# A transformer layer with 32 experts on one core: the test for further rounds turned round, and the second expert pair's work in another order

## What is computed

```python
def moe(h, w_router, b_router, w_up, b_up, w_down, b_down):
    ...
    top_vals, top_idx = lax.top_k(logits, TOP_K)          # 4 of 32 for each of 256 tokens
    wts = jax.nn.softmax(top_vals, axis=-1)
    ...
    def expert(acc, xs):
        wu, bu, wd, bd, g = xs
        gu = x @ wu + bu                                   # 1024 -> 2 x 1024
        gate, up = gu[:, :D_FF], gu[:, D_FF:]
        gate = jnp.minimum(gate, SWIGLU_LIMIT)
        up = jnp.clip(up, -SWIGLU_LIMIT, SWIGLU_LIMIT)
        glu = gate * jax.nn.sigmoid(SWIGLU_ALPHA * gate)
        y = ((up + 1.0) * glu) @ wd + bd                   # 1024 -> 1024
        return acc + g[:, None] * y, None
```

## Time and profile before

| | |
|---|---|
| runs | 1178.0, 1182.4, 1183.23 us; median 1182.4 us |
| profiled execution | 1181.97 us |
| its span, first to last instruction | 1180.2 us |
| TensorE busy | 1072.3 us (91%) |
| mean DMA rate over the span | 389 GB/s, 459.64 MB |
| mean granted TensorE clock | 0.979 of full |

### The profile page before, as it was taken

How to read it: one execution, slowest core, us unless ns; L and a number is a source line. 1 busy time by engine, 2 the same in 40 slices (tenths; PEclk the granted TensorE clock), 3 DMA queues, 4 the chain that set the end, 5 groups by cost and what they waited for, 6 DMA issues and landing times.

```text
span 1180.2 us, 13193 instructions
## 1 busy us (share of the span) xinstructions
PE 1072.3 (91%) x5399; PEld 505.3 (43%) x5399; DVE 304.6 (26%) x585; ACT 141.4 (12%) x275; POOL 43.2 (4%) x79
## 2 busy tenths in 40 slices
PE   7989999999999989898989898989898989898985
PEld 5755798554343333333333334333333343434321
DVE  3043867632212111111121211111212111212124
ACT  2013333111011010101010101010101010101011
POOL 2005000000000000000000000000000000000000
PEclk8999999999999999999999999999999999999998
DMA  9988564899999999999999999999999999999993
GB/s 331 407 304 274 192 257 138 345 422 385 429 427 430 428 427 429 429 429 428 427 428 429 429 428 428 429 428 429 429 428 429 429 429 428 428 429 422 420 421 123
DMA packets 51248, 459.64 MB, mean 389 GB/s; under 512 B 4444, under 2 KB 4504, under 8 KB 20648
## 3 DMA queue, kind: packets, MB, share of 16 engines
q1 hardware_dynamic: 49960, 455.12, 92.7%
q0 software_dynamic: 1024, 3.29, 1.0%
q10 hardware_dynamic: 224, 0.69, 0.2%
HBM read 457.51 MB, written 1.57 MB: 389 GB/s over the span
## 4 chain that ended last, share of the span: by engine, by line
PE 63%; DMA 32%; DVE 2%; issue 1%; SPq 1%; ACT 1%; POOL 0%; DVEq 0%; POOLq 0%; ACTq 0%
DMA ring<-in_w_down_dram 30%; PE ps L1605 17%; PE ps L1620 10%; PE ps L1555 6%; PE ps L1508 5%; PE ps L1519 5%; PE ps L1261 4%; PE ps L1475 2%; PE ps L1640 2%; PE ps L1548 1%; PE ps L1277 1%; PE ps L1535 1%; PE ps L1292 1%; PE ps L1294 1%; PE ps L1293 1%
## 5 line engine op out<-in xcount | busy, mean ns | idle before, releaser
L1605 PE MATMUL ps<-ring,arena 128*64 128x512 f32 x1664 | 364.8, 593 | 18.6 <-DMA ring<-in_w_up_dram 18.6
L1620 PE MATMUL ps<-ring,arena 128*64 128x512 f32 x896 | 212.8, 631 | 51.6 <-DMA ring<-in_w_down_dram 51.6
L1605 PEld LDWEIGHTS ps<-ring,arena 128*64 128x64 f32 x1664 | 121.3, 137 | 245.5 <-issue 243.2
L1620 PEld LDWEIGHTS ps<-ring,arena 128*64 128x64 f32 x896 | 73.5, 145 | 190.5 <-issue 169.6
L1115 DVE TENSOR_TENSOR arena<-ps,arena 128x512 f32<-128x512 f32 x64 | 44.0, 692 | 281.4 <-PE ps L1519 281.4
L1096 DVE TENSOR_SCALAR arena<-ps 128x512 f32<-128x512 f32 x32 | 20.6, 687 | 278.2 <-PE ps L1605 221.6
L1555 PE MATMUL ps<-ring,arena 128*64 128x512 f32 x368 | 80.8, 594 | 0.3 <-DMA ring<-in_w_up_dram 0.3
L1508 PE MATMUL ps<-arena 128*128 128x128 f32 x512 | 63.3, 282 | 0.0
L1508 PEld LDWEIGHTS ps<-arena 128*128 128x128 f32 x512 | 61.6, 196 | 1.8 <-issue 1.6
L1519 PE MATMUL ps<-arena 128*128 128x512 f32 x128 | 57.8, 594 | 1.2 <-ACT arena L716 1.2
L703 ACT ACTIVATE arena<-arena 128x512 f32<-128x512 f32 x32 | 19.6, 629 | 296.2 <-DVE arena L1096 296.2
(11 more groups left out here) (235 smaller groups left out, 801.7 us busy)
## 6 DMA issues: line engine op xcount, KB each, us to landing
ring<-in_w_up_dram SPq DMA_DIRECT2D x127, 2048.0 KB, 26.9
ring<-in_w_down_dram SPq DMA_DIRECT2D x63, 2048.0 KB, 23.1
ring<-in_w_in_dram SPq DMA_DIRECT2D x16, 1024.0 KB, 9.9
ring<-in_w_ada_dram SPq DMA_DIRECT2D x16, 1024.0 KB, 10.3
ring<-in_w_ada_dram SPq DMA_DIRECT2D x16, 512.0 KB, 11.8
ring<-in_w_out_dram SPq DMA_DIRECT2D x4, 1024.0 KB, 10.4
ring<-in_w_pa_dram SPq DMA_DIRECT2D x2, 1024.0 KB, 10.5
ring<-in_w_pb_dram SPq DMA_DIRECT2D x2, 1024.0 KB, 6.1
```

What stands on the lines that cost most here:

```text
L1605: ins = mm(ps[CAP * a:CAP * a + CAP, n, :], xgT[:, h, kk, CAP * a:CAP * a + CAP], w[a][:, n * HALF:(n + 1) * HALF], start=False, stop=(kk ...
L1620: ins = mm(ps[CAP * a:CAP * a + CAP, YB + n, :], hT[:, f, CAP * a:CAP * a + CAP], w[a][:, n * HALF:(n + 1) * HALF], start=(f == 0), stop=( ...
```

## The change

Two things are changed.

1. **The test for further rounds, on TensorE alone.** `further_rounds(pe, ...)`, four last products after it, becomes `finish(r)`: `If(flag < 1)` the last products (`last_scatter`), `Else` another round and `finish(r + 1)`. The other four engines keep their tests as they were.
2. **The first two pairs' order.** The second pair's `gather` leaves `up_first`. Its first half stands between the pairs, its second half before k-block 2 of the second pair. That pair's k-blocks 0 and 1 come before its bias: block 0 starts the banks (`start=first`), and the bias adds to them. `turn_hidden` moves from ahead of k-block 2 to ahead of k-block 3, `scatter(R)` from ahead of the bias to ahead of k-block 5, `turn_weights` from ahead of k-block 3 to ahead of k-block 7. On ScalarE the copy of the gather's second half moves behind the first pair's sigmoids.

```diff
-                for b in range(2):
-                    xg_out(R + 1, b, 1, SECOND[b])
+                xg_out(R + 1, 0, 1, SECOND[0])
                 sigmoids(R)
+                xg_out(R + 1, 1, 1, SECOND[1])
...
-                    if kk == 5:
-                        for b in range(2):
-                            gather(R + 1, b, SECOND[b])
...
+            def up_second(Q, chunk):
+
+                pe.wait_ge(u_read, Q + 1)
+                for kk in range(KB):
+                    if kk % 4 == 0:
+                        pe.wait_ge(xg_ready, Q * 2 + (kk // 4 + 1))
+                    if kk == 2:
+                        gather(Q, 1, SECOND[1])
+                        up_bias(Q, False)
+                    if kk == 3:
+                        pe.wait_ge(xg_ready, Q * 2 + 2)
+                        turn_hidden(Q - 1, FIRST_HB)
+                    if kk == 5:
+                        pe.wait_ge(hTe_ready, Q * 2)
+                        scatter(Q - 1)
+                    if kk == 7:
+                        turn_weights(Q - 1)
+                    up_block(1, kk, both_experts(chunk(kk), 2 * FF), kk == 0).then_inc(moe_free, 1)
...
-                pe.wait_ge(xg_ready, R * 2 + 4)
-                scatter(R)
-                up_by_block(R + 1, at(N + FIRST_UP), True)
+                gather(R + 1, 0, SECOND[0])
+                up_second(R + 1, at(N + FIRST_UP))
...
-                pe.wait_ge(woT_ready, 1 + (r + 1) * PAIRS)
-            further_rounds(pe, more, run)
-            pe.wait_ge(woT_ready, 1 + PAIRS)
-            for n in range(4):
-                t, c = n // 2, slice((n % 2) * HALF, (n % 2 + 1) * HALF)
-                pe.wait_ge(yg_ready, n + 1)
-                mm(ps[:, SB + n, :], woT[:, t, :], yg[:, t, c], start=True, stop=True).then_inc(last_scat, 1)
+
+            def last_scatter(r):
+                pe.wait_ge(woT_ready, 1 + r * PAIRS)
+                for n in range(4):
+                    t, c = n // 2, slice((n % 2) * HALF, (n % 2 + 1) * HALF)
+                    pe.wait_ge(yg_ready, n + 1)
+                    mm(ps[:, SB + n, :], woT[:, t, :], yg[:, t, c], start=True, stop=True).then_inc(last_scat, 1)
+
+            def finish(r):
+                if r == ROUNDS:
+                    last_scatter(r)
+                else:
+                    with pe.If(more[r - 1] < 1):
+                        last_scatter(r)
+                    with pe.Else():
+                        run(r)
+                        finish(r + 1)
+
+            finish(1)
```

More of the change, by code:

```diff
@@ L1540, in both_experts, with up_bias @@
                 return [v[:, a * 2 * FF:a * 2 * FF + n] for a in range(2)]
-            def up_bias(Q):
+            def up_bias(Q, first=True):
                 pe.wait_ge(u_read, Q + 1)
@@ L1548, in up_bias, with up_block @@
                         mm(ps[CAP * a:CAP * a + CAP, n, :], selbuf[:, a, :], bparts[:, n * HALF:(n + 1) * HALF],
-                           start=True, stop=False)
-            def up_block(h, kk, w):
+                           start=first, stop=False)
+            def up_block(h, kk, w, first=False):
                 for n in range(4):
@@ L1555, in up_block @@
                         ins = mm(ps[CAP * a:CAP * a + CAP, n, :], xgT[:, h, kk, CAP * a:CAP * a + CAP],
-                                 w[a][:, n * HALF:(n + 1) * HALF], start=False, stop=(kk == KB - 1))
+                                 w[a][:, n * HALF:(n + 1) * HALF], start=first, stop=(kk == KB - 1))
                 return ins
@@ L1574, in up_first, with up_last @@
                         up_block(0, kk, [spare[:, a, :] for a in range(2)]).then_inc(first_used, 1)
-            def up_by_block(Q, chunk, first):
+            def up_second(Q, chunk):
[15 more added lines that the diff above has]
+                    up_block(1, kk, both_experts(chunk(kk), 2 * FF), kk == 0).then_inc(moe_free, 1)
+            def up_last(Q, chunk):
                 pe.wait_ge(xg_ready, Q * 2 + 2)
-                if not first:
-                    pe.wait_ge(hTe_ready, Q * 2)
+                pe.wait_ge(hTe_ready, Q * 2)
                 up_bias(Q)
                 for kk in range(KB):
-                    if first and kk == 2:
-                        pe.wait_ge(acc_done, (Q - 1) * 4 + 2)
-                        turn_hidden(Q - 1, FIRST_HB)
                     if kk == 3:
-                        if first:
-                            pe.wait_ge(hTe_ready, Q * 2)
                         turn_weights(Q - 1)
@@ L1687, in experts @@
                 Q, n0 = R + PAIRS - 1, n0 + PC
-                up_by_block(Q, at(n0), False)
+                up_last(Q, at(n0))
                 pe.wait_ge(acc_done, Q * 4)
```

## The result

The changed kernel takes 1173.06 us (median of 6 runs, 1172.27 to 1174.36), the kernel before 1181.54 us (median of 6, 1178.0 to 1183.78). The ratio is 0.9926, 95% interval 0.9911 to 0.994: 0.74% faster, 8.7 us by the ratio and 8.5 by the medians. The profiled execution takes 1174.36 us against 1181.97, 7.6 us less.

A forecast was written before the change was run, and what follows sets the result against it. From about 300 us the stream of weights was taken to set the time. 1181.97 less 5.3 (branch) and 2.3 (order) gave 1174.4 us for the profiled execution; median forecast 1174.5, range 1171 to 1178.5.

The forecast's parts named there:

- The branch: TensorE ahead of the last products: not taking the branch removes an instruction-fetch stall and slow clock, gain 5.3 us.
- The clock term: Last products on TensorE: with the idle 4.08 us gone the clock stays up, 3.70 us instead of 5.37.
- The 0.3 us allowed for wait and test: TensorE ahead of the last products: time still left for waits, test and start, 0.3 us.
- The branch behind the last products: TensorE after the last products: taken branch costs about 4.1 us, ends near 1170.7, hidden; cost 0, cover 4 us.
- The order: First two pairs: slots freed earlier close a hole in the weight stream near 290 us, gain 2.3 us.
- The thirteenth transfer: Third pair's first weight transfer: issued at 347.5 against a limit of 347.9, so just in time.
- The sign of being wrong: 4 us of "issue" still ahead of the last products, or a GB/s dip near 348 or in the first pair.
- ScalarE's later table load: ScalarE in the second pair: the 1.28 us load ends at 283.0 and stays hidden, with 7 us of cover.
- The wait ahead of block 0: TensorE before the second pair's first k-block: a new wait of 0.8 us.
- the moved hole: Rival, chance 0.12: the stream stops at the third pair's first slot instead, only the branch pays: 1176.7 us.
- the falling clock: Rival, chance 0.10: the clock falls anyway, last products or blocks before them still cost 1.7 us: 1176.2 us.
- a stall that stays: Rival, chance 0.12: the test empties what was fetched ahead whichever way it goes, only the stream pays: 1179.7 us.

The follow-up runs named there:

- e1: Kernel before with only the turned test and last products of the change, first two pairs as before; ratio 0.9961, 1176.1 us.
- e3: Kernel before with the wait for `y_done` and raising of `moe_free` moved into the further rounds' code, taken branch kept; ratio 0.9962, 1176.6 us.
- e12: Changed kernel plus one more test ahead of the turned one, its taken branch skipping one semaphore instruction; ratio 0.9934 to the kernel before, 1174.1 us.
- e4: Kernel before with nine useless products between the wait for `y_done` and the test; ratio 0.9983, 1179.2 us.
- e10: Changed kernel with the wait for `y_done` and raising of `moe_free` moved into the further rounds' code; ratio 0.9930 to the kernel before, 1172.8 us.
- e2: Kernel before with only the new order of the first two pairs and on ScalarE, test as before; ratio 0.9976, 1178.0 us.
- e5: Changed kernel run again unaltered, on the chip of three other runs; ratio 0.9927 to the kernel before, 1173.3 us.
- e7: Kernel before with the scatter moved to ahead of the second pair's k-block 5, `turn_hidden` and `turn_weights` after it; ratio 1.0009, 1182.5 us.
- e8: Changed kernel with seven useless products, about 3.1 us, between the first two pairs; ratio 0.9954 to the kernel before, 1176.3 us.
- e11: Changed kernel with the second pair's bias ahead of k-block 0 instead of behind k-block 1; ratio 0.9936 to the kernel before, 1174.1 us.
- e9: Changed kernel with the scatter back between the pairs behind the half gather, `y_done` wait moved into further rounds' code; ratio 0.9945 to the kernel before, 1175.7 us.

## Why the prediction was right, and where a term was off

**The branch, 5.3 us forecast: 5.3 us measured** (tail 36.26 to 30.93; e1 the same). Each step holds. The stall is the fetch of far code behind a taken branch: it goes when the branch is not taken (e1), shrinks when the branch is reached earlier (e3), and a taken branch to near code costs 0.27 us (e12). The records say the same: 3.71 us taken and far, 0.22 taken and near, 0.08 not taken. The rule of the Trainium skill named in the prediction ("Runtime: NRT & Kernel Launch", "Instruction fetch mechanics") makes just this difference between near and far targets, and e12 agrees with it; "Advanced Engine Details and Errata", section "Control Flow Timing", gives some 0.11 us for a compare-and-branch, where here the near taken one took 0.22 and one not taken 0.08. The clock term holds as well (e4: 1.6 us without touching the stall). The 0.3 us allowed for wait and test measured 0.45; e10 shows that they go with the wait for `y_done`. The 0.1 us that I took off for the norm's steps was not lost: from VectorE's last additions to the store it is 3.83 us in both traces.

**The branch behind the last products, 0 us.** Nothing on the path moved. The fetch stands behind the start of the last products, and the tail has no room for a hidden cost: it is shorter by just what VectorE's additions gained. The branch ends at 1165.6, not near 1170.7 as in the sum, since the sequencer reaches it while the last products are still being worked on.

**The order, 2.3 us forecast: 2.9 us measured** (stream: 883.2 to 883.6 us in the kernel before, e1, e3 and e4, 880.3 to 880.7 in the changed kernel, e2, e5 and e10; the timed e2 gives 2.8, with 1.5 to 4.1 in its interval). The hole was there and is closed, as forecast. But the 2.9 us are not made up as the sum has them, and that they lie so near to 2.3 is in part luck. These are the times from the landing of the last ring transfer of the first pair (292.16 before, 292.85 after) to later landings, in us:

| landing of the | before | changed | gained |
|---|---|---|---|
| first behind it | 6.8 | 4.9 | 1.9 |
| fourth | 22.6 | 19.6 | 3.0 |
| thirteenth | 66.7 | 63.8 | 2.9 |
| fifteenth | 76.5 | 74.6 | 1.9 |
| 167th | 821.1 | 819.5 | 1.6 |
| 168th | 827.5 | 824.5 | 3.0 |

The first row is the late landing that I had counted, 1.9 to 2.0 us. In the kernel before a second delay of 1.1 us follows with the fourth transfer:

```profile
303.12 0.33 SPq L330 DMA_DIRECT2D ring<-in_w_down_dram  x1
...
ring<-in_w_down_dram SPq DMA_DIRECT2D x1, 2048.0 KB, 11.7
...
q8 instruction: 1, 0.02, 6.5%
```

It landed at 314.79, 6.0 us behind the third; the last row is the instruction queue between 310 and 311. My sum had no such term. Nor had it the 1.0 us that the changed kernel gives back at the fifteenth, behind the dip near 350. What is left by then, 1.6 to 1.9 us, is what closing the hole was worth in these two traces; over all traces of the two orders named above, counted from the half gather, it is 1.9 to 2.3 at the nineteenth and 1.5 to 2.2 at the 167th. The rest came over 700 us later: in the kernel before the 168th transfer landed 6.4 us behind the one before it, though it had been issued 33.6 us before. In e1, e3, e4 and e7, all with `up_by_block` in the second pair, it was 0.8 to 1.4 us late as well; in the changed kernel, e2, e5 and e8 to e11 it was 0.2 at most. But in e12, with the new order, it was 1.6 us late. So whether this part belongs to the order is not shown.

**What such late landings have in common.** In the thirteen traces, from the second pair on, 24 transfers that had been issued 10 us or more before they were due landed over 5.3 us behind the one before. In 23 of these intervals the instruction queue q8 moved a 16 KB packet, which held one of the 16 DMA engines for about 1.0 us (the 6.5% and 6.2% of the two q8 rows above are a sixteenth). But in 107 other intervals such a packet passed and the landing kept step. So the fetches are the likely cause of the second delays, and not the shown one: no run took a fetch away or moved it alone.

**The thirteenth transfer, "just in time".** It was issued at 348.92, 0.4 us later against the rest of this trace than in the sum, and landed 0.1 us late. The sign of being wrong that the prediction names, a dip near 348 and a stretch under 400 GB/s, was seen (339). With the 1.0 us given back two transfers later the passage was not free, and the sum had no price for it; the forecast's range was wide enough.

**ScalarE's later table load, hidden.** `turn_hidden` starts at 296.21 with no wait ahead of it.

**The wait ahead of block 0, 0.8 us forecast:** 0.73.

Of the rivals, the moved hole was there in a mild form, costing 1.0 us; neither the falling clock nor a stall that stays was seen. The sum, 1174.4 for the profiled execution, met 1174.36, and that is luck: stream and tail together were 8.6 us shorter, not 7.6, and the changed kernel's execution came to its half gather 1.0 us later. Against the forecast median, 1174.5, the measured one was 1.4 us lower.

What was wrong is in the expectations behind it: twice (e7, e11) I misjudged a wait in which GpSimd's table follows VectorE's reading, too short with nothing ahead of it, too long with a half gather ahead of it, and in e9 I took a lead of 7.9 us between issue and due landing for enough at every transfer. e9's first such transfer kept step with a lead of 8.2, a later one with 8.1 landed 2 us late; in e8 leads of 8.4 and 8.9 were 0.7 and 0.8 us short. The prediction's limits use the same 7.9 us and so were too generous; in the changed kernel the first eight transfers had leads of over 10 us, so it did not matter there.

## What to carry to other kernels

As far as these runs go, a rarely taken path belongs behind the common one, above all on an engine that others wait for: the far branch cost 3.6 us net and, through the clock, 1.7 more. Where that can't be written, reach the branch while work is still queued. And where a prefetched stream begins to be paced by the slots that the first steps free, the order of work between two freed slots counts as much as the work itself; look at what each piece covers on other engines before moving it.

## What was not expected of the hardware

- A stream with few transfers outstanding is slow before it is idle: in the changed kernel at 348 us the engines are busy 0.95 of the time at 339 GB/s, where a full queue gives 1.01 at 428.
- TensorE's sequencer ran only 2.8 us ahead of its array at the far branch (e3), less than one k-block of work, which is 3.5.
- GpSimd's small table copy takes 0.81 us where VectorE's product of the hidden rows (L1104) is under way as it starts, and 0.29 us where VectorE stands still. In e7 VectorE goes on at 288.18; in e11 it waits for ScalarE until 284.75. In the kernel before one copy, at 1009.88, took 0.29 us with VectorE's product starting 0.06 us behind it, so it is the copy's start that counts. GpSimd's rows, e7 first, then e11:

```profile
288.21 0.81 POOL L501 COPY selbuf<-sel 96x128 bf16<-96x128 bf16 x1 [42.42 <-DVE arena L1098]
```

```profile
282.52 0.29 POOL L501 COPY selbuf<-sel 96x128 bf16<-96x128 bf16 x1 [35.80 <-DVE arena L1098]
```

- The time to the first expert pair varies between executions by some 6 us (the second half gather starts at 252.69 in e5, at 258.98 in e12), while the stream behind it varies by 0.4 us among kernels of one order, e12 apart. So the spread of the timed runs probably comes mostly from the first part; with one trace for each kernel this is not shown.
